# The modulation's products, from the stick-breaking stage into the slots of the sparse attention

## The reference

```python
sh1, sc1, g1, sh2, sc2, g2 = jnp.split(
    (jax.nn.silu(c) @ ada_w[layer] + ada_b[layer])[:, None, :], ADA_CHUNKS, axis=-1)
csh1, csc1, cg1, csh2, csc2, cg2 = jnp.split(
    jax.nn.silu(c_ctx) @ ada_w[layer] + ada_b[layer], ADA_CHUNKS, axis=-1)
```

## Time and profile before

| what | us |
|---|---|
| median of 3 runs | 3607.01 (3599.83 to 3609.54) |
| the profiled execution | 3603.41 |
| its span, first to last instruction | 3602.0 |
| TensorE busy | 3346.2 (93%) |
| VectorE busy | 2274.6 (63%) |
| ScalarE busy | 1306.5 (36%) |
| GpSimd busy | 801.3 (22%) |
| mean granted clock of TensorE | 0.953 |

### The profile page before, as it was taken

How to read it: one execution, slowest core, us unless ns; L and a number is a source line. 1 busy time by engine, 2 the same in 40 slices (tenths; PEclk the granted TensorE clock), 3 DMA queues, 4 the chain that set the end, 5 groups by cost and what they waited for, 6 DMA issues and landing times. The chain is left out here.

```text
span 3602.0 us, 45108 instructions
## 1 busy us (share of the span) xinstructions
PE 3346.2 (93%) x17156; PEld 2775.1 (77%) x17156; DVE 2274.6 (63%) x4384; ACT 1306.5 (36%) x2285; POOL 801.3 (22%) x751
## 2 busy tenths in 40 slices
PE   7999899999999999999899899866889999999998
PEld 5555446888866678887677677766889999999998
DVE  4773334646555556464554435898768888888886
ACT  2343222323333343232444223324863333343433
POOL 1001222000100020002200002366853333333341
PEclk9678999999999999999899999988999999999999
DMA  3002232222211122332111222243569899899893
GB/s 134 12 7 90 106 123 82 94 100 94 94 60 47 47 71 96 99 102 78 56 56 50 71 88 84 82 154 112 213 260 322 309 313 322 309 324 315 306 314 127
DMA packets 180454, 515.17 MB, mean 143 GB/s; under 512 B 14992, under 2 KB 75408, under 8 KB 175120
## 3 DMA queue, kind: packets, MB, share of 16 engines
q1 hardware_dynamic: 128256, 305.70, 24.7%
q0 software_dynamic: 40464, 160.45, 13.0%
q10 hardware_dynamic: 11520, 46.15, 3.3%
HBM read 477.10 MB, written 35.13 MB: 142 GB/s over the span
## 5 line engine op out<-in xcount | busy, mean ns | idle before, releaser
L231 PE MATMUL bank<-h_hi,w_hi 128*128 128x512 f32 (+1 forms) x2528 | 972.6, 385 | 76.1 <-ACT w_hi L199 21.6
L231 PE MATMUL bank<-h_lo,w_hi 128*128 128x512 f32 (+1 forms) x2528 | 956.4, 378 | 0.0
L205 DVE TENSOR_TENSOR w_lo<-w_raw,w_hi 128x1024 fp32r<-128x1024 f32 (+1 forms) x468 | 598.9, 1280 | 333.0 <-ACT w_hi L199 327.4
L199 ACT ACTIVATE w_hi<-w_raw 128x1024 fp32r<-128x1024 f32 (+1 forms) x508 | 545.9, 1075 | 541.5 <-PE bank L231 527.4
L231 PE MATMUL bank<-h_hi,w_lo 128*128 128x512 f32 (+1 forms) x2528 | 601.6, 375 | 15.8 <-POOL w_lo L212 15.8
L231 PEld LDWEIGHTS bank<-h_hi,w_hi 128*128 128x128 f32 x2528 | 488.5, 193 | 159.5 <-issue 44.3
L231 PEld LDWEIGHTS bank<-h_lo,w_hi 128*128 128x128 f32 x2528 | 490.0, 194 | 63.6 <-issue 7.7
L231 PEld LDWEIGHTS bank<-h_hi,w_lo 128*128 128x128 f32 x2528 | 463.1, 191 | 83.4 <-POOL w_lo L212 17.0
L231 PE MATMUL bank<-e_hi,w_hi 128*128 128x384 f32 x1024 | 345.5, 337 | 5.9 <-DVE e_lo L2258 5.9
L231 PE MATMUL bank<-e_lo,w_hi 128*128 128x384 f32 x1024 | 344.2, 336 | 0.0
L2167 POOL DMA_INDIRECT own_row<-in_u_rows,own_e x128 | 157.7, 1232 | 321.4 <-DVE sums L2295 277.3
(11 more groups left out here) (405 smaller groups left out, 4804.2 us busy)
## 6 DMA issues: line engine op xcount, KB each, us to landing
w_raw<-in_w SPq DMA_DIRECT2D x476, 512.0 KB
ada_w<-in_ada_w POOLq DMA_DIRECT2D x24, 1024.0 KB, 5.1
expert_weights<-G ACTq DMA_DIRECT2D x12, 2048.0 KB, 7.2
Gin<-expert_weights SPq DMA_DIRECT2D x32, 768.0 KB
w_raw<-in_w SPq DMA_DIRECT2D x32, 704.0 KB
hidden_ahead<-u_stage ACTq DMA_DIRECT2D x40, 192.0 KB, 3.4
ahead<-hidden_ahead SPq DMA_DIRECT2D x20, 384.0 KB
na_bias<-in_bias ACTq DMA_DIRECT2D x4, 896.0 KB, 4.6
```

The source lines that it names most:

```text
L199: sc.activation(w_hi[s][:, 0:n], w_raw[raw_slot[u]][:, 0:n], ACT.Copy).then_inc(*w_hi_made.next(u))
L205: ve.tensor_tensor(w_lo[s][:, 0:n], w_raw[raw_slot[u]][:, 0:n], w_hi[s][:, 0:n], ALU.subtract).then_inc(*w_lo_made.next(u))
L231: m = te.matmul(out, wt, moving, start=(not low and k == 0 and moving is hi), stop=(low and k == len(blocks) - 1))
```

## The change

The modulation leaves `stick` and enters `nsa`. `ada_tensor(g)` does half a step's sums (4 matmuls) in each slot from 2 to 47, and all 8 of the first step in slot 1. The turn of a step stands on even slots, ahead of the next sums. The sums go into the linear bank of the head pair whose query projection was taken out of it; the turns of six steps lie side by side in the same bank and VectorE adds the bias of all six in one instruction at slots 12, 24, 36 and 48. The query projection two pairs on, which uses that bank, now waits for that addition. There are two row buffers. The weights of all 24 steps are fetched by GpSimd in `nsa`, from the end of the projections on, two ahead. The silu of `c` is made from a sigmoid on ScalarE and a product on VectorE, beside the gates' sigmoid, so the silu table is no longer loaded. The three `scaled_g` instructions move from the end of `stick` to the end of `nsa`.

```diff
@@ -619,6 +618,8 @@
+        silu = sb(st, "silu_c", [P, KT, 2])
+        ada_in = [loaded(f"ada_in{b}") for b in range(2)]
...
@@ -629,6 +630,8 @@
+        ada_w = [sb(st, f"ada_w{b}", [P, KT, 256]) for b in range(2)]
+        rows_of = [sb(st, f"ada_rows{b}", [2, 256]) for b in range(2)]
...
@@ -701,6 +704,7 @@
+            sc.activation(silu[:, :, :], col("c", 0, 16).rearrange("p (k c) -> p k c", c=2), ACT.Sigmoid).then_inc(*act.next("sigmoid c"))
...
@@ -738,6 +742,8 @@
+            ve.wait_ge(*act.at("sigmoid c"))
+            ve.tensor_tensor(silu[:, :, :], silu[:, :, :], col("c", 0, 16).rearrange("p (k c) -> p k c", c=2), ALU.mult).then_inc(*dve.next("silu"))
...
@@ -769,6 +775,41 @@
+        def ada_tensor(g):
+            k, half = divmod(g, 2)
+            sums = lin[UQ[k // 6] % 2][0:2, 0:256]
+            if half == 0:
+                te.wait_ge(*ada_in[k % 2].at(k))
+                if k % 6:
+                    te.wait_ge(*dve.at("ada rows", k - 1))
+            for c in range(4 * half, 4 * half + 4):
+                m = te.matmul(sums, silu[:, c, :], ada_w[k % 2][:, c, :], start=(c == 0), stop=(c == KT - 1))
+            if half:
+                m.then_inc(*pe.next("ada", k))
+
+        def ada_turn(k):
+            te.wait_ge(*dve.at("ada rows", k))
+            at = 256 + 4 * (k % 6)
+            for n in range(2):
+                m = te.matmul(lin[UQ[k // 6] % 2][:, at + 2 * n:at + 2 * n + 2], rows_of[k % 2][:, n * P:(n + 1) * P], ident[0:2, 0:2], start=True, stop=True)
+            m.then_inc(*pe.next("ada turned", k))
...
+        def ada_rows(k):
+            ve.wait_ge(*pe.at("ada", k))
+            if k >= 2:
+                ve.wait_ge(*pe.at("ada turned", k - 2))
+            ve.tensor_copy(rows_of[k % 2][:, :], lin[UQ[k // 6] % 2][0:2, 0:256]).then_inc(*dve.next("ada rows", k))
+
+        def ada_vector(p):
+            ve.wait_ge(*pe.at("ada turned", 6 * p + 5))
+            bias = col("ada_b", 12 * p, 12).unsqueeze(2).to_broadcast([P, 12, 2])
+            ve.tensor_tensor(mod[:, 12 * p:12 * p + 12, :], lin[UQ[p] % 2][:, 256:280].rearrange("p (n c) -> p n c", c=2), bias,
+                             ALU.add).then_inc(*dve.next("mod", p))
+            bank_of.taken(UQ[p], dve)
...
@@ -802,6 +843,10 @@
+                if 0 < g <= slots and g % 2 == 0:
+                    ada_turn(g // 2 - 1)
+                for n in range(2) if g == 1 else (g,) if 1 < g < slots else ():
+                    ada_tensor(n)
...
@@ -854,6 +899,8 @@
+                if 0 < g <= slots and g % 2 == 0:
+                    ada_rows(g // 2 - 1)
...
@@ -877,10 +924,24 @@
+                if g and g % 12 == 0:
+                    ada_vector(g // 12 - 1)
...
+            ve.wait_ge(*dve.here())
+            for s in range(3):
+                chunk, c, name = ((1, 0, "norm1"), (1, 1, "norm1"), (4, 0, "norm2"))[s]
+                ve.scalar_tensor_tensor(scaled_g[:, s, :], mod[:, chunk * KT:(chunk + 1) * KT, c], 1.0, col(name, 0, KT), ALU.add, ALU.mult).then_inc(*dve.next("scaled_g"))
+
+        def gpsimd():
+            after(gp, "nsa projections")
+            for k in range(N_ADA // 2):
+                if k >= 2:
+                    gp.wait_ge(*pe.at("ada", k - 2))
+                gp.dma_start(ada_w[k % 2][:, :, :], io["ada_w"][k]).then_inc(*ada_in[k % 2].next(k))
...
@@ -940,43 +1002,12 @@
-        silu = sb(st, "silu_c", [P, KT, 2])
-        rows_of = sb(st, "ada_rows", [2, 256])
-        ada_w = [sb(st, f"ada_w{b}", [P, KT, 256]) for b in range(2)]
-        ada_in = [loaded(f"ada_in{b}") for b in range(2)]
...
-        def ada_sums(k):
-            te.wait_ge(*ada_in[k % 2].at(k))
-            if k == 0:
-                te.wait_ge(*act.at("silu"))
-            else:
-                te.wait_ge(*dve.at("mod", k - 1))
-            for c in range(KT):
-                m = te.matmul(x_bank[0:2, 0:256], silu[:, c, :], ada_w[k % 2][:, c, :], start=(c == 0), stop=(c == KT - 1))
-            m.then_inc(*pe.next("ada", k))
...
-        def ada_rows(k):
-            ve.wait_ge(*pe.at("ada", k))
-            ve.tensor_copy(rows_of[:, :], x_bank[0:2, 0:256]).then_inc(*dve.next("ada rows", k))
...
-        def ada_add(k):
-            ve.wait_ge(*pe.at("ada turned", k))
-            bias = col("ada_b", 2 * k, 2).unsqueeze(2).to_broadcast([P, 2, 2])
-            ve.tensor_tensor(mod[:, 2 * k:2 * k + 2, :], x_bank[:, 256:260].rearrange("p (n c) -> p n c", c=2), bias, ALU.add).then_inc(*dve.next("mod", k))
...
@@ -1005,10 +1036,6 @@
-                if m < steps:
-                    for a in range(6 * p + (n * 3) // 2, 6 * p + ((n + 1) * 3) // 2):
-                        ada_sums(a)
-                        ada_turn(a)
...
@@ -1027,8 +1054,6 @@
-            sc.preload_act_table_set("silu_and_others")
-            sc.activation(silu[:, :, :], col("c", 0, 16).rearrange("p (k c) -> p k c", c=2), ACT.Silu).then_inc(*act.next("silu"))
...
@@ -1090,30 +1115,13 @@
-                    for a in range(6 * p + (n * 3) // 2, 6 * p + ((n + 1) * 3) // 2):
-                        ada_rows(a)
-                        ada_add(a)
...
-            for s in range(3):
-                chunk, c, g = ((1, 0, "norm1"), (1, 1, "norm1"), (4, 0, "norm2"))[s]
-                ve.wait_ge(*dve.at("mod", ADA_STEPS - 1))
-                ve.scalar_tensor_tensor(scaled_g[:, s, :], mod[:, chunk * KT:(chunk + 1) * KT, c], 1.0, col(g, 0, KT), ALU.add, ALU.mult).then_inc(*dve.next("scaled_g"))
...
-            def ada_fetch(k):
-                if k >= 2:
-                    gp.wait_ge(*pe.at("ada", k - 2))
-                gp.dma_start(ada_w[k % 2][:, :, :], io["ada_w"][k]).then_inc(*ada_in[k % 2].next(k))
-
-            ada_fetch(0)
-            ada_fetch(1)
-            fetched = 2
...
@@ -1135,10 +1143,6 @@
-                if m < steps:
-                    while fetched < min(ADA_STEPS, 2 + 6 * p + ((n + 1) * 3) // 2):
-                        ada_fetch(fetched)
-                        fetched += 1
```

More of the change, by code:

```diff
@@ L32 @@
 N_ADA = 6 * KT
-ADA_STEPS = N_ADA // 2
 HK = 128
@@ L891, in nsa @@
         vector()
+        gpsimd()
         ended("nsa")
@@ L952, in place @@
             return p, n, slice(lo, T), slice(lo + P, T), slice(lo, lo + P)
-        def ada_sums(k):
-            te.wait_ge(*ada_in[k % 2].at(k))
-            if k == 0:
-                te.wait_ge(*act.at("silu"))
-            else:
-                te.wait_ge(*dve.at("mod", k - 1))
-            for c in range(KT):
-                m = te.matmul(x_bank[0:2, 0:256], silu[:, c, :], ada_w[k % 2][:, c, :], start=(c == 0), stop=(c == KT - 1))
-            m.then_inc(*pe.next("ada", k))
-        def ada_turn(k):
-            te.wait_ge(*dve.at("ada rows", k))
-            for n in range(2):
-                m = te.matmul(x_bank[:, 256 + 2 * n:258 + 2 * n], rows_of[:, n * P:(n + 1) * P], ident[0:2, 0:2], start=True, stop=True)
-            m.then_inc(*pe.next("ada turned", k))
-        def ada_rows(k):
-            ve.wait_ge(*pe.at("ada", k))
-            ve.tensor_copy(rows_of[:, :], x_bank[0:2, 0:256]).then_inc(*dve.next("ada rows", k))
-        def ada_add(k):
-            ve.wait_ge(*pe.at("ada turned", k))
-            bias = col("ada_b", 2 * k, 2).unsqueeze(2).to_broadcast([P, 2, 2])
-            ve.tensor_tensor(mod[:, 2 * k:2 * k + 2, :], x_bank[:, 256:260].rearrange("p (n c) -> p n c", c=2), bias, ALU.add).then_inc(*dve.next("mod", k))
         def tensor():
```

## The result

The changed kernel takes 3549.61 us (median of 4 runs, 3548.50 to 3550.53) against 3608.28 us for the kernel before in the same session: 0.9842 of the time, 95% interval 0.9825 to 0.9859. By the medians that is 58.7 us less; the forecast was 28 us less. The profiled execution took 3549.85 us, its span is 3548.4 us, 53.6 us shorter than the span of before, and its mean granted clock is 0.964.

The account below looks back on a forecast made before the run. TensorE was taken to bound both stages, the slots at a granted clock of 0.71. The stick-breaking stage's -93 and the slots' +65 gave -28 us, a median of 3579 us, range 3545 to 3622.

Parts of the forecast that it names:

- the main case: Whole kernel: the forecast of 3579 us with its own range 3560 to 3596, chance 0.55.
- rival C: Slots and after: the clock is 1.00 throughout, +54 - 108 = -54 us, kernel 3553 us; chance 0.11.
- What bounds the slots: Sparse-attention slots: TensorE sets the pace, busy 208.03 of 214.10 us; an added matmul has next to nothing to hide in.
- (a): Slots: the sums and turns of 24 steps add 101 us, more bursts 2 us: +103 us at full clock.
- (b): Start of the slots: TensorE waits for the first weights, fetched only after the projections: +4 us, from 2 to 6.
- (c): Slots: the added matmuls cover TensorE's 6.1 us of gaps: -6 us, 0 if none of it.
- (d): Slots: the added matmuls lift the mean clock from 0.71 to 0.95: -36 us.
- The bound of +54: Slots: the low bound of their +65 us sum, with the clock at 1.00 throughout, 47 us saved for 36.
- What leaves the stage, and what it keeps: Stick-breaking stage: 123.0 us of modulation leave; 1, 10, 12 and 7 us are given back: -93 us.
- (e): Slots: VectorE's added copies and additions and later fetches cost nothing; 8 us if the turn waits for copies.
- A: Slots keep their low clock and last 344 us; kernel 37 us slower, 3644 us; chance 0.10.
- D: Slots: the 22 later fetches take 12 us instead of about 6, +44 us, kernel 3623 us; chance 0.05.

Follow-up runs that it names:

- the 188 useless ones: Kernel before, with four useless matmuls over 128 rows added to each of slots 1 to 47: 3630.14 us, ratio 1.0067.
- the early fetch: Changed kernel, with the modulation's first weight fetch no longer waiting for the end of the projections: 3545.96 us, ratio 0.9840.
- The run with 2 rows: Kernel before, with four useless matmuls in each of slots 1 to 47, contracting over 2 rows instead of 128: 3789.97 us, ratio 1.0509.
- whole steps: Changed kernel, with a whole modulation step (8 matmuls) in every second slot instead of a half step in each: 3566.92 us, ratio 0.9898.
- 3, 3 and 2: Changed kernel, with 16 steps in the slots, each spread as 3, 3 and 2 matmuls over three slots, and 8 in the stick-breaking stage's last pair: 3559.10 us.
- 4, 4, none spread: Changed kernel, with 16 steps in the slots, each as 4, 4 and no matmuls over three slots, and 8 in the stick-breaking stage's last pair: 3572.17 us.

## Why the prediction was right, and where it was off

The direction, the mechanism and both stages' signs were right, and 3549.61 us lies in the stated range of 3545 to 3622. It lies near its lower end, though, and outside 3560 to 3596, which I had given the main case: that the result is in the range owes to the room left for rival C. The gain is twice what I wrote. By the steps of the prediction:

- **What bounds the slots.** Right: TensorE, with nothing to hide in. The matmuls added there cost 0.44 us each, the full price, once the clock was level.
- **(a) +103.** 192 matmuls at 0.44 us are 85 us, and the slots are 257.6 - 240.85 = 16.8 us longer than with the 188 useless ones, of which 4 matmuls are 1.8, the first fetch 2.9 and the turns the remaining 12: together 97, as an estimate. Off by 6, since I added up durations whose ends overlap with the next instruction, and 2 us for bursts.
- **(b) +4.** 2.9 us, once; the early fetch took it off.
- **(c) and (d), -6 and -36.** This is the step that failed in size. Together they are -57 us (215.1 against 157.8), of which the gaps are some -4 and the clock -53, where I had -36. I took 0.62 for the time of the slots' work at full clock over that at half, from one pair of slots; by the whole stretch, 124 us at the lower level cost some 53, which is 0.57. And I kept 10% of the time at the lower level, where the trace has 0.82 up to 110 us and 1.00 from there to the end of the slots. The bound of +54 assumed the ratio of 0.62 at a clock of 1.00, so the slots at +42.6 lie below it. The run with 2 rows, almost wholly at 0.50, gives nearly the same ratio: there the slots' own instructions are busy 410.45 - 161.5 (the added ones) = 249 us, against 238.52 - 90.4 = 148 with 128 rows, 0.59.
- **What leaves the stage, and what it keeps.** -98.3 for -93. The first three pairs give 219.2 - 131.8 = 87.4 us where 18 of 24 steps were 92.3: 4.9 given back, and I had 8. The last pair lasts 36.2 us, which is what the sum of 27.6 for the chain and some 9 for the clock says; with the 1.4 us by which the end behind it grew, 20 us are given back there for the 22 of the forecast. The waits for GpSimd's masks came as forecast, if shorter (1.2 to 1.8 us a tile, where I had 2 to 3), and so did the clock of 0.64.
- **(e)** No wait for the copies (0.0 us before L795), none for the addition, none for later fetches. The cover was needed, though: with whole steps the addition showed 3.7 us, and with 3, 3 and 2 the copies 5.1 us. That they cost nothing holds for this spread, with a half step in every slot.

Of the rivals, C (the clock at 1.00 throughout, 3553 us, chance 0.11) is the nearest, nearer than the forecast of 3579. It holds for the slots but not for the stage, whose last pair lost its clock as in the main case; the slots, better than its +54, made up for that. A needed 0.83 or less in the slots; it is the mechanism that whole steps and the 4, 4, none spread brought about (0.93 and 0.87). The change as made misses it by having something in every slot. D didn't show: the fetches land in 5.0 to 7.4 us, 5.1 in the median, beside a VectorE that is busier than before.

The reading of the skill's rule is now shown rather than argued. The Trainium skill (TensorE: Matmul & The Clock Gate, "Part 1: The HAM clock gate") says that the clock is set by how busy the engine has been. The traces here don't agree with it if busy means the engine's busy time: it was busy for 410.45 of 412.66 us at a clock of 0.53, and for 238.52 of 240.85 us at 0.99, in streams that differ only in the rows of the added matmuls.

## What to carry to other kernels

Read the granted clock of a stretch before pricing work that goes into it: if TensorE is saturated there and still at the lower level, matmuls over all 128 rows, put evenly into every turn of the loop, may cost half their price or less (here 43 of 100 us), and where they are moved from a place with spare time they are worth moving. Spread them so that no turn is without; the same work in every second or in two of three turns lost 15 and 19 us here. And look at the place they leave: where they were the only thing that kept the engine going, its waits and its lower clock come back (here 20 of the 31 us that six steps took).

## What the runs showed of the hardware

- The granted clock changed with the rows of the added matmuls, at the same busy share. The same stream of instructions, with four added matmuls of 256 moving columns and 2 stationary ones in each slot, ran at 0.99 with 128 rows, 0.80 with 64 and 0.53 with 2. The lift from 0.71 to 0.99 came with two stationary columns.
- Useless matmuls can pay: 94 of them made the kernel 0.4% faster (interval 0.3 to 0.6%), and 16 in the last pair took that pair from 36.2 to 29.9 us, too little to show in the kernel's time.
- With 64 rows the slots ran at 0.50 from 150 to 180 us and at 1.00 from 210 us on.
- A busy engine at the lower level looks the same in the busy column as one at the upper. Only the clock column and the durations (3.57 for 1.89 us) tell.
